# 64 bytes left free between the transposed activations and the tiles behind them in a float32 three-block kernel

## The reference, cut to what matters

```python
def swiglu(x, w_in, w_out):                       # d_ff = 2816
    a, b = jnp.split(x @ w_in, 2, axis=-1)
    return (jax.nn.silu(a) * b) @ w_out

x = x + 0.5 * swiglu(rms_norm(x, ffn1_norm[l]), ffn1_w_in[l], ffn1_w_out[l])   # first block
x = x + 0.5 * rms_norm_2(swiglu_2(h, ffn1_w_in[l], ffn1_w_out[l]), ffn1_norm_post[l])  # the two layers
```

## Time and profile before

| | |
|---|---|
| median of three runs | 1826.59 us (1824.67 to 1831.79) |
| the profiled execution's own time | 1829.37 us |
| its span, first to last instruction | 1827.3 us |
| TensorE matmul / weight load busy | 1790.4 us (98%) / 1656.0 us (91%) |
| VectorE / ScalarE / GpSimd busy | 1060.1 us (58%) / 911.7 us (50%) / 45.3 us (2%) |
| read from HBM | 326.8 MB |

### The profile page before, as it was taken

The page is one execution under the profiler, slowest core; times in us unless marked ns, Lnnn a source line. Parts: engine busy times, 40 slices in busy tenths (PEclk is TensorE's granted clock), DMA queues, the critical chain, the costliest instruction groups (busy, mean ns, idle before and its releaser), DMA issues.

```text
span 1827.3 us, 33276 instructions
## 1 busy us (share of the span) xinstructions
PE 1790.4 (98%) x13114; PEld 1656.0 (91%) x13114; DVE 1060.1 (58%) x1393; ACT 911.7 (50%) x1180; POOL 45.3 (2%) x66
## 2 busy tenths in 40 slices
PE   8999998999999999999999999999999999999998
PEld 8999877999999999888898999899999888989997
DVE  5554686645464556666676544555464657675454
ACT  5444565443344445476755444443454567644443
POOL 0000120000000000000000000000000000000000
PEclk9999999999999999999999999999999999999999
DMA  7555423555465555443354555555546442445552
GB/s 311 203 188 189 176 108 116 207 199 191 170 241 189 201 184 190 179 164 136 136 188 162 196 184 178 210 201 190 185 158 232 165 181 94 162 150 208 193 197 93
DMA packets 47856, 329.19 MB, mean 180 GB/s; under 512 B 5392, under 2 KB 5648, under 8 KB 9616
## 3 DMA queue, kind: packets, MB, share of 16 engines
q1 hardware_dynamic: 44496, 316.84, 47.9%
q10 hardware_dynamic: 3264, 11.03, 1.8%
HBM read 326.80 MB, written 1.05 MB: 179 GB/s over the span
## 4 chain that ended last, share of the span: by engine, by line
issue 82%; PE 13%; ACT 2%; POOL 1%; DVE 1%; DMA 0%; DVEq 0%; POOLq 0%; ACTq 0%
PE work L1496 3%; PE work L1495 3%; PE work L1497 3%; POOL rstd L552 1%; PE acc L1497 1%; PE acc L1495 1%; PE acc L1496 1%; DMA pre<-pre 0%; ACT prob L720 0%; PE acc L1588 0%; PE work L1554 0%; DVE lo L1003 0%; ACT hi L601 0%; ACT squared L621 0%; PE acc L1714 0%
## 5 line engine op out<-in xcount | busy, mean ns | idle before, releaser
L1003 DVE TENSOR_TENSOR lo<-raw,hi 128x2048 fp32r<-128x2048 f32 x280 | 640.0, 2292 | 468.2 <-ACT hi L601 467.8
L1495 PE MATMUL work<-xT_hi,hi 128*128 128x256 f32 x2752 | 768.1, 279 | 6.8 <-DVE lo L1003 6.4
L1497 PE MATMUL work<-xT_hi,lo 128*128 128x256 f32 x2752 | 763.7, 277 | 0.0
L1496 PE MATMUL work<-xT_lo,hi 128*128 128x256 f32 x2752 | 763.6, 277 | 0.0
L601 ACT ACTIVATE hi<-raw 128x2048 fp32r<-128x2048 f32 x280 | 534.2, 1911 | 233.8 <-PE work L1497 191.2
L1495 PEld LDWEIGHTS work<-xT_hi,hi 128*128 128x128 f32 x2752 | 518.8, 189 | 17.3 <-DVE lo L1003 8.2
L1496 PEld LDWEIGHTS work<-xT_lo,hi 128*128 128x128 f32 x2752 | 519.0, 189 | 2.5
L1497 PEld LDWEIGHTS work<-xT_hi,lo 128*128 128x128 f32 x2752 | 518.6, 188 | 0.0
L1497 PE MATMUL acc<-hi,hT_lo 128*128 128x512 f32 x480 | 189.2, 394 | 0.0
L1496 PE MATMUL acc<-lo,hT_hi 128*128 128x512 f32 x480 | 188.3, 392 | 0.0
L1495 PE MATMUL acc<-hi,hT_hi 128*128 128x512 f32 x480 | 187.1, 390 | 0.0
(11 more groups left out here) (262 smaller groups left out, 1944.4 us busy)
## 6 DMA issues: line engine op xcount, KB each, us to landing
raw<-stream SPq DMA_DIRECT2D x298, 1024.0 KB, 4.8
pre<-pre ACTq DMA_DIRECT2D x7, 512.0 KB, 5.8
mem_in<-mem ACTq DMA_DIRECT2D x3, 1024.0 KB, 5.8
post<-post ACTq DMA_DIRECT2D x6, 512.0 KB, 3.8
x<-x SPq DMA_DIRECT2D x2, 512.0 KB, 5.1
pre<-pre SPq DMA_DIRECT2D x2, 512.0 KB, 3.7
out<-x SPq DMA_DIRECT2D x4, 256.0 KB, 2.0
alibi<-alibi ACTq DMA_DIRECT2D x1, 768.0 KB, 15.3
```

Source lines behind the costliest of these rows:

```text
L1003: nc.vector.tensor_tensor(lo[:, s, :], raw[:, s, :], hi[:, s, :].bitcast(F32), ALU.subtract).then_inc(lo_ready, 1)
L1495: nc.tensor.matmul(dst, a_hi, b_hi, start=start, stop=False)
L1496: nc.tensor.matmul(dst, a_hi, b_lo, start=False, stop=False)
L1497: return nc.tensor.matmul(dst, a_lo, b_hi, start=False, stop=stop)
```

## The change

```diff
         params = new("params", [P, max(B1P_N, LP_N)])
         xT_hi = new("xT_hi", [P, KD, T], F32R)
         xT_lo = new("xT_lo", [P, KD, T], F32R)
+        room(64)
         pre = new("pre", [P, D])
         post = new("post", [P, D])
         r_memk = room(4096)
```

## The result

The kernel with the 64 bytes takes **1845.82 us**, the median of five runs (1844.64 to 1847.32), beside 1826.59 us for five runs of the kernel before (1823.98 to 1831.79). The ratio is 1.0104, with a 95% interval of 1.0087 to 1.012. The forecast of "same", 1827 us in a range of 1818 to 1836, is wrong: it is slower by 19.2 us.

A forecast was written before the change was run, and what follows sets the result against it. The prediction took TensorE's matmul distance as the bound (busy 1790.4 of 1827.3 us). Every term was 0, added to the profiled 1829.4 us; set to the runs' median, this gave 1827 us, range 1818 to 1836.

The forecast's parts named there:

- same: Whole kernel: no change beyond about 0.5% (9.1 us), likeliest 1827 us; chance 0.87.
- the first: Channel products on xT, 2752 x 3 of 13,114 matmuls: all operands keep their addresses, so cost 0.
- a few stretches of 20 us outside the loops: Rival: stretches swap their pace, 0.7 us each, 2 to 3 us for a few; 1824 to 1830 us, chance 0.15.
- The same two-layer comparison: Second feed-forward part's start: 173 matmuls in 20 us in the first layer, 179 in the second, 3.4% apart.
- The 512-column products: 2016 matmuls whose stationary operand moves from 64 to 0 modulo 128: taken as 0, bounds 32 us less, 16 us more.
- the weight load alone is indifferent to the place: Reason for 0 on 512-column products: loads take 189 ns at 0 and 188 ns at 64 modulo 128.
- Moving operands: br and memT in channel products and the attention's tiles, going from 64 to 0 modulo 128: cost 0.
- ScalarE and VectorE: Their instructions on moved tiles: equal times at 0 and 64 modulo 128, cost 0 to 2 ns each.
- GpSimd's powers: Powers at each seam, 0.92 and 0.54 us, difference read as the values' doing: 0, bounds 6.8 us less, 4.6 more.
- The slower rival: Feed-forward rows units: 512-column products fall into the slow pace, 16 us more, 1843 us; chance 0.06.
- the channel products, whose operands keep their place, take another pace throughout a feed-forward loop: Sign in the profile after, in the feed-forward loops, that would prove the prediction wrong; ten of 256 columns were expected in 1.13 us.

The follow-up runs named there:

- last_from_xt: Kernel after, but the last matmul of each rows unit takes its weights from xT_lo (64) instead of hT_lo (128), computing other values: 1826.55 us, 0.9984 of before.
- end_apart2: Kernel before with hT at 128 and a second copy of the last rows matmul's weights in a tile at 64: 1824.06 us, 0.9959 of before.
- only_ht: Kernel before with only the 4 KB room of hT moved, from 64 to 128 modulo 256: 1844.63 us, 1.0089 of before.
- xt_zero: Kernel before with only xT moved, from 64 to 128 modulo 256: 1872.98 us, 1.0245 of before.
- kick: Kernel after plus a 64-column identity matmul ahead of the first channel unit of each chunk but the first: 1861.81 us, 1.0178 of before.
- shift128: The change with 128 bytes left free in place of 64: 1844.89 us, 1.0083 of before.
- but_ht_256: Kernel after, but the room of hT stays at 64 modulo 256 as before: 1836.55 us, 1.0054 of before.

## Why the prediction was wrong

**The step that failed** is the first: "Moving operand, stationary operand and accumulator all keep their addresses ... and they cost what they did: 0." It took a matmul's time for a function of that matmul's own operands. In the loop the channel products have two paces on the same addresses, 113.6 and 117.8 ns. Which one they take is handed over by what runs ahead, and the last matmul's weights at 64 or 128 were enough to choose (**last_from_xt**, **end_apart2** against **only_ht**). The term of 0 for this group measured 21.7 us in the loops (610.6 us for 588.9), of which the rows units gave back enough to leave 18.4.

The trace of before held a warning, and the text read it too narrowly: the same code at two paces was priced as a few stretches of 20 us outside the loops, on the ground that the pace "is settled by something other than the address". In the loops it is settled by where the operands of the rows unit ahead lie. And whatever is repeated was settled the same way each time: here 54 times out of 54. The price was in the trace of before too. `br` lies at 64 like `xT`, and the last 192 channel matmuls on it, in both layers, run at the slow pace:

```profile
922.26 0.28 PE L1495 MATMUL work<-br_hi,hi 128*128 128x256 f32 x1
...
944.75 0.28 PE L1497 MATMUL work<-br_hi,lo 128*128 128x256 f32 x1
```

(944.75 - 922.26) / 191 = 117.7 ns, 4% over the 113 ns of the earlier trace rows. At that pace the 54 channel stretches, 5184 matmuls, cost some 22 us more, and the term of 0 would have had a price to be weighed against.

What settles the stretches outside the loops stays open. The same two-layer comparison still stands in the kernel after, with 172 matmuls in 20 us and 179 on the same code:

```profile
982.00:1002.00 20.00, 20.00 (x172) 1.00 0.57 200
1654.00:1674.00 20.00, 20.00 (x179) 1.00 0.56 204
```

**The 512-column products** were the disputed term, with bounds of -32 and +16 us around 0. Those on `hT`, 1440 of the 2016, measured -4.0 us: 227 for 229 ns at `hT` on 128, and 233 at 192, 232 at 0. The reason "the weight load alone is indifferent to the place" holds for the duration of a load of `hT`, here after the change beside the earlier trace rows, and not quite for those of the weights:

```profile
L1498 PEld LDWEIGHTS work<-xT_hi,lo 128*128 128x128 f32 x2752 | 525.4, 191 | 0.0
...
L1496 PEld LDWEIGHTS acc<-hi,hT_hi 128*128 128x128 f32 x480 | 90.1, 188 | 16.4
```

A load of `hT` stays at 188 ns while its matmuls come 1% closer and those behind the unit 4% further apart. Of the three loads of a channel step, whose addresses stayed, the third went from 188 to 191 ns, and the loads under `memT` went from 188 to 192. So a load's row is no measure of what its own address costs, and a few ns on it are a mark of the slower pace. The Trainium skill (TensorE: Matmul & The Clock Gate, Step-by-step: what each phase is for) says that loading the next weights takes no read bandwidth from the running matmul, through a port of its own. The runs here show a dependence that this sentence would not lead one to expect: with nothing moved but `xT`, the stream, from 64 to 128, the weights' own place, the matmuls' distance went from 113.6 to 120 ns (**xt_zero**).

**Moving operands, "Cost 0".** `br` and `memT` went to the weights' own place and took 120 ns, where before `memT` took 113.4 and `br` 113.4 or 117.8. Eight steps of `br` after, 0.12 us each:

```profile
948.83 0.28 PE L1496 MATMUL work<-br_hi,hi 128*128 128x256 f32 x1
...
949.79 0.28 PE L1498 MATMUL work<-br_hi,lo 128*128 128x256 f32 x1
```

By the groups, the 64 x 3 matmuls on `memT` went from 277 to 283 ns, 1.2 us, and the 176 x 3 on `br` from 148.5 to 149.8 us busy, 1.3 us. The comparison with the earlier trace rows misled because there the weight tile is the stream and the stationary block another tile with 30 columns: one operand at the new place, not the pair of places that the change makes.

**What held.** ScalarE and VectorE cost 0: 1908 ns for 2048 elements, 1224 ns for 1024 on tiles now at 0 modulo 128. GpSimd's powers kept 0.92 and 0.54 us though their columns moved, so it is not the address modulo 128 that parts them:

```profile
L946 ACT ACTIVATE merge<-merge 128x2048 f32<-128x2048 f32 x6 | 11.4, 1908 | 0.0
...
L1285 DVE TENSOR_TENSOR lru_y<-lru_m,lru_g 128x1024 f32<-128x1024 f32 x1 | 1.2, 1224 | 0.0
```

```profile
698.54 0.92 POOL L553 TENSOR_TENSOR rstd<-var,neg_half 128x1 f32<-128x1 f32 x1 [2.65 <-DVE var L1019]
700.58 0.54 POOL L553 TENSOR_TENSOR rstd<-var,neg_half 128x1 f32<-128x1 f32 x1 [1.12 <-DVE var L1019]
```

**The slower rival** named 1843 us, close to the time, and the meeting of two operands in one place, and it still isn't what happened: it put the slow pace in the rows unit, which got faster. The size agrees because the price was the difference of the two paces in which the kernel was seen to run, and the chance of 0.06 was too small for a pace already seen to vary on fixed addresses. Of the signs that the prediction named as proving it wrong, "the channel products, whose operands keep their place, take another pace throughout a feed-forward loop" is the one that came.

## What to carry to other kernels

Where TensorE runs back to back, the distance of its matmuls is a result to be measured for the whole sequence, and an edit of addresses is no edit without effect: here the stream's place modulo 256 bytes, with the weights at 128, is worth up to 2.4%, and one weight load at the end of a unit 1%. Look for one kind of operation that shows two paces in one trace, on the same operands or on operands at the same place; if there is one, price any change near it at the difference of the paces times *all* matmuls of the loop, not of one stretch. When comparing address variants, keep the pair of operands, the order and what runs ahead the same, and treat the tile that ends a unit as a knob of its own.

## What the runs showed of the hardware that was not expected

- 256 columns have three paces from start to start: 113.5, 117.8 and 120 ns; 512 columns have about 227 to 233 ns. All are at the full granted clock.
- 256 bytes is a period for the tiles behind `xT`, and 128 is none: `room(256)` gives 1.0001 with the paces of before, `room(128)` 1.0083.
- With the weights at 128, a stream at 64 has two paces that keep themselves up for 96 matmuls, and even past a short other matmul (**kick**). The rows unit ahead chooses, and moving its last weight load from 128 to 64 is enough to change the choice; with the whole unit at 192 the pace turns over each time. A stream at 192 had 117.8 ns in the loops and 113.3 on `br` in **shift128**. A stream at 128 takes 120 ns, behind `hT` at 64 and at 128 alike, and a stream at 0 takes 120 ns in 52 of 54 stretches.
- No run moved the weights. Whether the stream's distance from them counts, or its place by itself, is not shown.
- What meets inside the chip (which lines or banks of the memory, or at which point of the load) was not measured and stays open, and so does the spread of **but_ht_256**.
